# A hybrid decoder block on one core: shared-memory regions at new offsets, eight buffers for value rows, gate products begun six units earlier, and the final normalisation split between two engines

## What is computed

```python
def peer(h, w_query, sub_keys, expert_u, expert_v):
    q = (hf @ w_query).reshape(T, PEER_HEADS, 2, PEER_HALF)
    s = einsum('thpd,hpkd->thpk', q, sub_keys)
    s1, i1 = top_k(s[:, :, 0], 16); s2, i2 = top_k(s[:, :, 1], 16)
    ...                                   # the best 16 sums of the 16 x 16 pairs: idx, best
    gate = softmax(best)
    act = einsum('td,thkd->thk', h, expert_u[idx])
    out = einsum('thk,thkd->td', gate * gelu(act), expert_v[idx])

x = x + peer(rmsnorm(x, g_ffn), ...)
return rmsnorm(x, g_final)                # y = x * rsqrt(mean(x^2) + 1e-6) * g
```

## Time and profile before

| | us |
|---|---|
| median of 3 runs (4323.43 to 4324.79) | 4324.64 |
| the profiled execution, its own time | 4327.3 |
| the profiled execution, span of the core | 4325.6 |
| PE busy in it | 4260.9 |
| DVE / ACT / POOL busy | 1925.8 / 1419.7 / 2358.8 |

### The profile page before, as it was taken

One profiled execution on the slowest core, in us unless ns is written; L12 is line 12 of the kernel. 1 busy time (PEld: TensorE's weight loads), 2 busy tenths in 40 slices (PEclk: granted clock), 3 DMA queues, 4 the chain that ended last, 5 costly groups with the idle time before them and its releaser, 6 DMA issues.

```text
span 4325.6 us, 53178 instructions
## 1 busy us (share of the span) xinstructions
PE 4260.9 (99%) x20393; PEld 3663.3 (85%) x20393; DVE 1925.8 (45%) x2504; ACT 1419.7 (33%) x1780; POOL 2358.8 (55%) x705
## 2 busy tenths in 40 slices
PE   8999999999999999999999999999999999999997
PEld 6888888877787888878999999999997777777776
DVE  2010035111112022048935766676746666666663
ACT  4222221233233122132344555555532222222222
POOL 3444433333343434433556676666767777777773
PEclk9999999999999999999999999999999999999998
DMA  4233322222223333222346888888877787788772
GB/s 165 97 119 120 119 98 87 92 84 78 87 87 141 119 112 124 97 78 87 133 146 256 324 321 329 318 332 320 323 299 299 299 314 304 303 314 315 305 291 112
DMA packets 201754, 859.75 MB, mean 199 GB/s; under 512 B 16784, under 2 KB 98768, under 8 KB 111312
## 3 DMA queue, kind: packets, MB, share of 16 engines
q1 hardware_dynamic: 62928, 458.26, 28.9%
q0 software_dynamic: 36864, 268.45, 15.7%
q10 hardware_dynamic: 101888, 132.23, 8.6%
HBM read 795.96 MB, written 62.91 MB: 199 GB/s over the span
## 4 chain that ended last, share of the span: by engine, by line
PE 94%; POOL 2%; DVE 1%; ACT 1%; issue 1%; DMA 1%; ACTq 0%; SPq 0%; DVEq 0%; POOLq 0%
PE bank L1574 17%; PE bank L1576 17%; PE bank L1575 17%; PE bank L1598 8%; PE twin L1598 8%; PE twin L1862 4%; PE twin L1866 4%; PE twin L1864 4%; PE bank L1862 4%; PE bank L1866 4%; PE bank L1864 4%; POOL low L460 2%; PE twin L1833 1%; DVE wide L1474 1%; PE twin L1576 1%; PE twin L1574 1%
## 5 line engine op out<-in xcount | busy, mean ns | idle before, releaser
L460 POOL TENSOR_TENSOR low<-raw,high 128x2048 fp32r<-128x2048 f32 x432 | 2005.1, 4641 | 1778.5 <-ACT high L531 1777.5
L531 ACT ACTIVATE high<-raw 128x2048 fp32r<-128x2048 f32 x432 | 828.5, 1918 | 2352.6 <-PE bank L1576 1153.4
L1574 PE MATMUL bank<-x_high,high 128*128 128x384 f32 (+1 forms) x3680 | 1324.8, 360 | 6.2 <-POOL low L460 6.2
L1576 PE MATMUL bank<-x_high,low 128*128 128x384 f32 (+1 forms) x3680 | 1321.3, 359 | 0.0
L1575 PE MATMUL bank<-x_low,high 128*128 128x384 f32 (+1 forms) x3680 | 1320.9, 359 | 0.0
L1574 PEld LDWEIGHTS bank<-x_high,high 128*128 128x128 f32 x3680 | 691.5, 188 | 71.4 <-POOL low L460 4.4
L1576 PEld LDWEIGHTS bank<-x_high,low 128*128 128x128 f32 x3680 | 691.3, 188 | 63.9
L1575 PEld LDWEIGHTS bank<-x_low,high 128*128 128x128 f32 x3680 | 691.5, 188 | 63.3
L1862 PE MATMUL twin<-high,a_high 128*128 128x512 f32 x768 | 304.2, 396 | 5.4 <-POOL low L460 5.4
L1862 PE MATMUL bank<-high,a_high 128*128 128x512 f32 x768 | 304.0, 396 | 3.0 <-POOL low L460 3.0
L1866 PE MATMUL bank<-high,a_low 128*128 128x512 f32 x768 | 304.2, 396 | 0.0
(11 more groups left out here) (221 smaller groups left out, 4782.2 us busy)
## 6 DMA issues: line engine op xcount, KB each, us to landing
raw<-weights SPq DMA_DIRECT2D x433, 1024.0 KB, 4.8
act_dram<-act_out ACTq DMA_DIRECT2D x128, 192.0 KB, 4.1
retrieved_dram<-stage ACTq DMA_DIRECT2D x48, 512.0 KB, 6.6
act_in<-act_dram ACTq DMA_DIRECT2D x32, 768.0 KB, 7.7
gates_in<-retrieved_dram ACTq DMA_DIRECT2D x32, 768.0 KB, 9.1
gates_dram<-sgu_act ACTq DMA_DIRECT2D x32, 256.0 KB, 2.1
gate_in<-gates_dram ACTq DMA_DIRECT2D x32, 256.0 KB, 2.7
xa<-x SPq DMA_DIRECT2D x4, 1024.0 KB, 9.1
```

What stands on the lines that cost most here:

```text
L460: nc.gpsimd.tensor_tensor(low[:, slot, :], raw[:, slot, :], high[:, slot, :].bitcast(F32), ALU.subtract).then_inc(low_done, 1)
L531: nc.scalar.activation(high[:, slot, :], raw[:, slot, :], ACT.Copy).then_inc(high_done, 1)
L1574: nc.tensor.matmul(o, high[:, slot, w], x_high[:, 0:tiles, k, :], start=(k == 0), stop=False)
L1576: ins = nc.tensor.matmul(o, low[:, slot, w], x_high[:, 0:tiles, k, :], start=False, stop=(k == KT - 1))
```

## The change

`LEAD` falls from 24 to 16 and `TURN = 2` comes in: PE turns the indices behind unit 15, runs two more units, and takes the first gate step behind unit 18 (`FIRST_STEP = 18`), its 19th. `TRAIL` becomes 14. POOL waits for `listed_done` behind its `low_part` of unit 17, and fetches at most one row of `expert_u` in each of units 17 to 19 and two in later ones. The value rows get eight buffers; the four new ones lie in `x_high` and `x_low`, which are free once the expert stage is over. In the transition ACT's wait for its own stores (`act_stored`) moves behind two `high_part`. The last normalisation takes its square root with a bias (as `root` did elsewhere), has DVE multiply the first 1024 columns by `gfin` ahead of time (`gained`), and then splits the scaling: ACT the first 1024 columns (`scale_first`), DVE the other 1024 (`last_scale`). It is done for tile 3 within the last group, and for the others between DVE's last three additions. The base becomes a multiple of 512 bytes and the small block 1.75 KB (1792 bytes), so that `region_c` starts at a multiple of 256.

```diff
+VALUE_BUFS = 8
-LEAD = 24
-TRAIL = ETILES - LEAD - STEPS * STAGES
+LEAD = 16
+TURN = 2
+FIRST_STEP = LEAD + TURN
+TRAIL = ETILES - FIRST_STEP - STEPS * STAGES
...
-        place = [nc.sbuf_base + 31 & ~31]
+        place = [nc.sbuf_base + 511 & ~511]
-        small = room(2.15625)
+        small = room(1.75)
...
+            def fetch_v(slot):
+                b = slot % VALUE_BUFS
+                if slot >= VALUE_BUFS:
+                    pool.wait_ge(rows_used, SLOTS + slot - VALUE_BUFS + 1)
+                elif b < ROW_BUFS:
+                    pool.wait_ge(rows_used, SLOTS - ROW_BUFS + b + 1)
+                else:
+                    pool.wait_ge(unit_done, AT["values"]["unit"])
+                fetch_row(expert_v, slot, b)
...
-                while fetched_v < SLOTS and fetched_v < sums_by(n) + ROW_BUFS - 1:
+                wanted = min(SLOTS, sums_by(n) + VALUE_BUFS // 2, fetched_v + 2)
...
-            for j in range(2):
-                act.wait_ge(act_stored[j], stored[j].now())
             act.wait_ge(al_done, lows.next())
             load_pair(2, 0)
             n_groups = ETILES // EG
             high_part()
             act.wait_ge(rows_used, SLOTS)
             nc.scalar.activation(slot_act[:], slot_act[:], ACT.Gelu).then_inc(slot_act_done, 1)
+            for j in range(2):
+                act.wait_ge(act_stored[j], stored[j].now())
             product_high(1)
...
                     if db == NB - 1:
                         act.wait_ge(evac[b], n)
-                        square_sum(t, 1, D - BW, D)
-                        if t > 0:
-                            last_root(t, t - 1)
-            last_root(DENSE_T, DENSE_T - 1)
+                        last_squares(t, 1, D - BW, D)
+                        last_root(t + 1, t)
+                        scale_first(t + 1, t)
+                        store(t + 1, t)
...
+                    if n == ETILES - 1:
+                        first_sum(t + 1, t)
+                        last_scale(t + 1, t)
...
+                if n == ETILES - 5:
+                    dve.wait_ge(gfin_in, 16)
+                    first_sum(0, DENSE_T)
+                    gained(DENSE_T)
+                if n == ETILES - 3:
+                    last_scale(0, DENSE_T)
+                    for t in range(DENSE_T):
+                        gained(t)
```

More of the change, by code:

```diff
@@ L300, in program @@
         gfin = at("gfin", [P, D], F32, region_x + 32 * 1024)
+        junk = [at(f"junk{t}", [P, D], F32, region_x + (t * 8 if t < DENSE_T else 48) * 1024) for t in range(TT)]
         bank = [ctx.enter_context(nc.psum_tensor(f"bank{b}", [P, BW], F32)) for b in range(2)]
@@ L388, in program @@
         listed_done = sem("listed_done")
-        rows_in = [sem(f"rows_in{b}") for b in range(ROW_BUFS)]
+        rows_in = [sem(f"rows_in{b}") for b in range(VALUE_BUFS)]
         rows_used = sem("rows_used")
@@ L480, in _, with fetch_row @@
                 low_part(0)
[L483 to L490, removed]
+            def fetch_row(table, slot, b):
                 nc.gpsimd.indirect_dma_start(
@@ L497, in _ @@
                 low_part((n + 1) % 2)
-                if n == LEAD:
+                if n == LEAD + 1:
                     pool.wait_ge(listed_done, 1)
-                if n >= LEAD:
-                    while fetched_u < SLOTS and fetched_u < dots_by(n) + ROW_BUFS - 1:
-                        fetch(expert_u, fetched_u)
+                if n > LEAD:
+                    wanted = min(SLOTS, dots_by(n) + ROW_BUFS - 1, fetched_u + (1 if n < LEAD + 4 else 2))
+                    while fetched_u < wanted:
+                        fetch_u(fetched_u)
                         fetched_u += 1
@@ L506, in _ @@
                 low_part((n + 1) % 2)
-                while fetched_v < SLOTS and fetched_v < sums_by(n) + ROW_BUFS - 1:
-                    fetch(expert_v, fetched_v)
+                wanted = min(SLOTS, sums_by(n) + VALUE_BUFS // 2, fetched_v + 2)
+                while fetched_v < wanted:
+                    fetch_v(fetched_v)
                     fetched_v += 1
@@ L927, in _ @@
             ins.then_inc(slots_kept, 1)
+            pairs(TURN // 2, LEAD)
             kept_stages = [Count(), Count()]
@@ L1478, in _ @@
             gate_hits(0)
-            for n in range(LEAD, ETILES):
-                at_step = n - LEAD
+            for n in range(FIRST_STEP, ETILES):
+                at_step = n - FIRST_STEP
                 if at_step + 1 < STAGES * STEPS:
@@ L1507, in _, with first_sum, gained, last_scale @@
             sums = 0
+            def first_sum(n, t):
+                dve.wait_ge(sq_done, 3 * TT + (1 if n == 0 else 2 + n))
+                nc.vector.tensor_scalar(norm_ms[:, t:t + 1], squares[:, 0, t:t + 1], 1.0 / D, EPS, ALU.mult,
+                                        ALU.add).then_inc(ms_done, 1)
+            def gained(t):
+                nc.vector.tensor_tensor(xb[:, t, 0:D // 2], xa[:, t, 0:D // 2], gfin[:, 0:D // 2], ALU.mult)
+            def last_scale(n, t):
+                dve.wait_ge(root_done, 2 * TT + n + 1)
+                nc.vector.reciprocal(norm_inv[:, t:t + 1], norm_root[:, t:t + 1]).then_inc(inv_done, 1)
+                dve.wait_ge(inv_done, n + 1)
+                nc.vector.scalar_tensor_tensor(out=xb[:, t, D // 2:D], in0=xa[:, t, D // 2:D],
+                                               scalar=norm_inv[:, t:t + 1], in1=gfin[:, D // 2:D], op0=ALU.mult,
+                                               op1=ALU.mult).then_inc(normed, 1)
             product(0)
@@ L1825, in _ @@
             ins.then_inc(slots_turned, 1)
+            for n in range(TURN):
+                column(n % 2, tiles=DENSE_T)
             made, outs = Count(), Count()
```

85 lines of the change are left out of this document (46 added, 39 removed).

## The result

The changed kernel takes 4256.8 us (median of 4 runs, 4255.8 to 4258.6), the kernel before 4324.7 (4323.4 to 4327.0) on the same chip: ratio 0.984, 95% interval 0.9828 to 0.9852, so 67.9 us less. The prediction said 4263.8, range 4256 to 4297, so faster for the reasons it gave, but it was 7 us short.

The account below looks back on a forecast made before the run. PE was taken to bound the kernel, through matmul distance, its few stalls and the end. Gains of 7.1, 1.6, 9.2, 12.7 and 30.2 sum to 60.8; 4325.6 less these, less 1.0, gives 4263.8 us, range 4256 to 4297.

Parts of the forecast that it names:

- The gate steps: Expert stage: the gate steps themselves would only move, 96 x 0.47 us before and after, so no gain.
- First gate step: PE's two waits at its first gate step and a slower product behind would all go: 7.1 us gained.
- Start of the value stage: PE's loss while ACT waited for its stores ahead of the second `high_part` would go: 1.6 us gained.
- Eight buffers: Value stage: PE's 13 stalls for `low`, in units where a second fetch waited for a buffer, would go: 9.2 us.
- My doubt about the cover: Value stage with eight buffers: two fetches make the low part 1.2 us late against a cover of 1.6; it holds.
- End: From T, end of unit 125, the end moves from T + 42.1 to T + 29.4: 12.7 us gained.
- the first `gained` at 5 us or more: Sign at the end: the first `gained` on DVE takes that long beside POOL's low part of 4.6 us.
- The two other signs: At the end: last store issued 12 us behind PE's last matmul, and some 17 us from there to the end.
- The rival without a contest: At the end, no port contest, `gained` goes ahead or between: 4259.7 us, or 4289.9 without the fast stage; no separate chance.
- Addresses: Value stage: aligning the stationary operand in `region_c` to 64 bytes takes 6.7 ns off each matmul: 30.2 us gained.

Follow-up runs that it names:

- b4: Changed kernel with ACT's wait for its own stores back ahead of the second `high_part` at the start of the value stage: 4258.4 us.
- c1: Changed kernel with each of the three last `gained` put behind the last addition of its own tile: 4254.8 us.
- d1: Changed kernel on the old base with a small block of 1856 bytes, stationary and moving operand 320 bytes apart modulo 512: 4291.6 us.
- a5: Changed kernel with the small block at 1728 bytes, stationary and moving operand 192 bytes apart modulo 512: 4267.5 us.
- a1: Kernel before the change with only the new base and the small block of 1.75 KB: 4300.0 us.
- a2: Changed kernel with the small block 32 bytes longer, so only `region_c` with `a_high` and `a_low` is 32 bytes off: 4287.8 us.
- a4: Changed kernel with base 32 bytes higher and small block 32 bytes shorter: `high` and `low` 32 off, `region_c` aligned: 4289.9 us.
- f1: The changed kernel run again unchanged, on one chip with f2: 4258.1 us.
- f2: The version with each `gained` behind its own tile's last addition, run again beside the changed kernel: 4254.2 us.
- e1: Changed kernel with `a_low` moved 32 bytes against `a_high`; in odd groups the second `a_high` moved too: 4282.3 us.
- b1: Changed kernel with four buffers for value rows again, fetched three rows ahead as before: 4276.2 us.

## Why the prediction was right or wrong

Three steps failed. The price of a stall: its wait was counted, and the matmuls behind it were taken at their usual pace; the runs showed 2.0 us more at the first gate step and 1.2 more in the value stage. The gate steps, taken to "only move": 1.9 us of excess went. And the reason for the address term, though its number held. Part by part:

- **First gate step, 7.1: right in place, 2.0 short.** The waits went as predicted. The step that failed is the price of a stall: I counted the stalled distances and 0.3 behind the last of them, and took the matmuls after that at their usual pace. They ran at half the clock and lost 1.6 us more, which the starts right behind the earlier trace rows would have told; the rest, 0.4, lies ahead of the first gate step, where the excess is 4.3 us before and 3.9 after, and its cause stays open.
- **Start of the value stage, 1.6: right in the trace**; alone, in the changed kernel, the move is worth only 0.5 (b4).
- **Eight buffers, 9.2: mis-sized, and not independent.** The slow first distance behind each stall (13 times 0.10) makes it 10.5 in the kernel before; the clock doesn't fall there. And with fast matmuls the four buffers lose 16.3: added last, the buffers bring 16.3, and added first, by the trace before, 10.5; the addresses the other way round. The sum of both is nearly the same, so this interaction explains no part of the miss, but a sum that had only one of the two would have failed by 6 us. My doubt about the cover (low part 1.2 late, cover 1.6) was too dark: two fetches took 3.5 us, and the low part is 0.14 late.
- **End, 12.7: measured 13.3.** There was a contest, and the first `gained` stood at 2.0 behind T, but the order within it was not as told. I had let the low part go first and all three `gained` behind it; the first `gained` went ahead in 1.22 us, and the second was the one held up, with 5.63. So the sign "the first `gained` at 5 us or more" came true for the second, and `gained` was done at T + 9.9 instead of 10.9, one `gained` sooner. PE lost nothing, and the store landed in 3.8 us instead of 4.0: the end stood at T + 28.4 instead of 29.4. The two other signs, a last store 12 us behind PE's last matmul and 17 us to the end, don't follow from the sum, which gives some 8 and 13; measured are 8.2 and 12.4. The rival without a contest is out; moving `gained` out of it (c1) brought 3.3.
- **Addresses, 30.2: measured 30.4, but the reason was wrong.** I had put it down to the stationary operand being 32 bytes off, and passed over the gate step, whose pace spoke against it. It is the distance between the two operands; 0 and 256 are free. The number came out by luck: the new distance happens to be 256, and other multiples of 64, which by my reason were as good, cost 33 to 35 us at 320 (d1) and 9 to 11 at 192 (a5).
- **Not in the sum.** The gate steps' 1.9 us of excess are gone in a1 as well, so addresses again; by which pair isn't settled: against the changed kernel a2 and a5 have -0.6, a4 1.3 and d1 2.5. And the first part of the run: 4.7 us in the two traces, of which little is the change. f1 and f2, the same program up to there, begin the expert stage at 2084.8 and 2081.5, and a1 at 2083.2. The medians (67.9 us) hold some 1 us of it, the terms behind that point 66.7.
- **Total.** 66.7 against 60.8: 2.0 and 1.2 mostly for what follows a stall, 1.9 for the gate steps, 0.6 for the end and 0.2 for the distance. The result lies at the low edge of the range, since I had bounded each term by its waits and none by what happens behind them.

## What to carry to other kernels

Put the stationary and the moving operand of a hot float32r matmul a multiple of 256 bytes apart, not only each at a round address: of the distances tried, 0 and 256 modulo 512 were free and the six others cost 2 to 7 ns per matmul. Here that was worth 30 us of 4325 (26 as the only change, a1), nearly as much as all the reordering put together (34). A stall's price is read from the starts of the matmuls until they are back at their usual distance, with the granted clock beside them, not from the wait alone; and when the bounding engine gets faster, read the stalls of the others again, for their cover has shrunk. An early piece of work with two SBUF inputs on DVE isn't free next to POOL: it is better late and beside ACT than early and in the way.

## What was new about the hardware

- Distance of float32r matmuls of 512 columns at a granted clock of 1.00: 226.7 ns with operands 0 or 256 bytes apart modulo 512, 228.9 at 192, 232.4 at 384, 233.3 at 160, 224, 288 and 320. The weight load's own time is 0.19 us in all.
- With only the third product's weights 32 bytes off (the even groups of e1), the two matmuls ahead of it slow down (232.3 and 239.0 ns), and it itself hardly (228.6). Not explained.
- Waits of 2.2 and 4.2 us with four matmuls between them took the granted clock to 0.50, and it stayed there for 11 to 14 matmuls of 384 columns behind them, 1.6 to 2.0 us lost in all; single waits of 0.5 to 1.7 us in the value stage left it at 1.00 (a1, b1).
- DVE's operations with two SBUF inputs and POOL's low part took turns: of three `gained` the first took 1.22 us, as alone, the low part beside it 5.69 instead of 4.6, the second `gained` 5.63, the third 1.22.
- Two executions of the same code differ by up to 3.3 us ahead of the expert stage. 1.6 of it is one stall, PE's wait for `x_low`, 4.5 us in most traces and 2.9 in two.
